# Attention products with the values as stationary operand, two heads side by side, and the softmax sums inverted once per attention

## The reference

```python
def one(qblk):                                   # first attention ("mla"), per 128 queries
    sc = einsum('bqhd,bkhd->bhqk', qblk, k) * scale
    p = softmax(sc, axis=-1)
    return einsum('bhqk,bkhd->bqhd', p, v)
...
s_win = s_win * scale + bias                     # second ("na"): a window of the tokens, and the context
p = softmax(concatenate([s_win, s_ctx], axis=-1), axis=-1)
return einsum(p_win, v_win) + einsum(p_ctx, vc)
...
ya = (oa * silu(za)) @ w_oa
yb = (ob * silu(zb)) @ w_ob
y = (sigmoid(ga) * ya + sigmoid(gb) * yb) @ w_out
```

## Time and profile before

| | |
|---|---|
| median of 3 runs | 3332.46 us (3329.71 to 3333.55) |
| the profiled execution | 3333.67 us, span 3331.9 us |
| PE busy | 3113.7 us, 93% of the span |
| PE weight loads busy | 2443.1 us, 73% |
| VectorE busy | 1628.2 us, 49% |
| ScalarE busy | 1123.6 us, 34% |
| DMA queue, share of 16 engines | 22.5% |
| chain that ended last | PE 86%, DVE 8%, ACT 3% |

### The profile page before, as it was taken

How to read it: one execution, slowest core, us unless ns; L and a number is a source line. 1 busy time by engine, 2 the same in 40 slices (tenths; PEclk the granted TensorE clock), 3 DMA queues, 4 the chain that set the end, 5 groups by cost and what they waited for, 6 DMA issues and landing times.

```text
span 3331.9 us, 38502 instructions
## 1 busy us (share of the span) xinstructions
PE 3113.7 (93%) x15469; PEld 2443.1 (73%) x15469; DVE 1628.2 (49%) x2719; ACT 1123.6 (34%) x1821; POOL 134.7 (4%) x145
## 2 busy tenths in 40 slices
PE   7999898999999899999999999679999989987998
PEld 6888745666666688887788888458888757877886
DVE  5434544555556554344743345765535435245335
ACT  3322223434344333233332233543323333233332
POOL 0000001211111100000000000000000000100000
PEclk9999899999999899999999999789999979987999
DMA  4333221111100133332233322013233210301231
GB/s 129 94 96 101 78 74 45 46 42 34 53 17 20 64 95 95 102 95 93 84 96 96 100 90 72 1 44 95 89 102 97 59 29 1 93 7 48 88 93 61
DMA packets 186183, 234.76 MB, mean 70 GB/s; under 512 B 14201, under 2 KB 127446, under 8 KB 185750
## 3 DMA queue, kind: packets, MB, share of 16 engines
q1 hardware_dynamic: 186006, 232.29, 22.5%
HBM read 228.05 MB, written 4.19 MB: 70 GB/s over the span
## 4 chain that ended last, share of the span: by engine, by line
PE 86%; DVE 8%; ACT 3%; issue 2%; POOL 1%; SPq 0%; DMA 0%; DVEq 0%; ACTq 0%
PE banks L866 61%; PE banks L991 3%; PE banks L1370 3%; PE banks L1023 2%; PE banks L977 1%; PE banks L1364 1%; PE banks L1358 1%; PE banks L1014 1%; PE banks L1058 1%; PE banks L1087 1%; PE banks L1083 1%; PE banks L955 1%; DVE diff_scores L2378 1%; DVE diff_small L2384 1%; PE banks L1032 1%
## 5 line engine op out<-in xcount | busy, mean ns | idle before, releaser
L1922 DVE TENSOR_TENSOR weights_lo<-weights_raw,weights_hi 128x1024 fp32r<-128x1024 f32 (+3 forms) x377 | 453.1, 1205 | 999.1 <-ACT weights_hi L1441 997.6
L866 PE MATMUL banks<-operand_hi,weights_hi 128*128 128x512 f32 x2080 | 822.6, 395 | 34.5 <-DVE weights_lo L1922 13.0
L866 PE MATMUL banks<-operand_hi,weights_lo 128*128 128x512 f32 x2080 | 815.8, 392 | 0.0
L866 PE MATMUL banks<-operand_lo,weights_hi 128*128 128x512 f32 x2080 | 815.8, 392 | 0.0
L1441 ACT ACTIVATE weights_hi<-weights_raw 128x1024 fp32r<-128x1024 f32 (+3 forms) x377 | 391.2, 1041 | 1060.4 <-PE banks L866 1030.1
L866 PEld LDWEIGHTS banks<-operand_hi,weights_hi 128*128 128x128 f32 x2080 | 394.1, 189 | 124.4 <-issue 27.2
L866 PEld LDWEIGHTS banks<-operand_lo,weights_hi 128*128 128x128 f32 x2080 | 394.4, 190 | 83.7 <-issue 2.2
L866 PEld LDWEIGHTS banks<-operand_hi,weights_lo 128*128 128x128 f32 x2080 | 393.9, 189 | 83.3
L866 PE MATMUL banks<-hidden_ffn_hi,weights_hi 128*128 128x512 f32 x352 | 137.1, 390 | 0.0
L866 PE MATMUL banks<-hidden_ffn_lo,weights_hi 128*128 128x512 f32 x352 | 136.9, 389 | 0.0
L866 PE MATMUL banks<-hidden_ffn_hi,weights_lo 128*128 128x512 f32 x352 | 136.9, 389 | 0.0
(11 more groups left out here) (519 smaller groups left out, 4520.5 us busy)
## 6 DMA issues: line engine op xcount, KB each, us to landing
weights_raw<-in_ffn_w_in_dram SPq DMA_DIRECT2D x352, 256.0 KB, 3.1
weights_raw<-in_ffn_w_out_dram SPq DMA_DIRECT2D x88, 512.0 KB, 3.8
weights_raw<-in_w_in_dram SPq DMA_DIRECT2D x36, 512.0 KB, 3.6
weights_raw<-in_rwkv_w_rkv_dram SPq DMA_DIRECT2D x24, 512.0 KB, 3.9
weights_raw<-in_w_mod_dram SPq DMA_DIRECT2D x24, 512.0 KB, 4.9
weights_raw<-in_w_kv_dram SPq DMA_DIRECT2D x16, 512.0 KB, 3.6
weights_raw<-in_rwkv_w_o_dram SPq DMA_DIRECT2D x8, 512.0 KB, 5.1
weights_raw<-in_diff_w_q_dram SPq DMA_DIRECT2D x8, 512.0 KB, 4.8
```

Of the source, the lines that this page charges most:

```text
L866: mm = nc.tensor.matmul(o, l, r, start=first and t == 0 and job["opens"], stop=last and t == 2, **skip)
L1922: nc.vector.tensor_tensor(ring_lo[0:p, u["slot"], 0:n, 0:w], ring_raw[0:p, u["ring"], 0:n, 0:w], f32(ring_hi[0:p, u["slot"], 0:n, 0:w]), A ...
```

## The change

For lanes 0 and 2, step 4 handles two heads: the values of a head (64 columns) are the stationary operand and the turned probabilities (128 queries) stream past them. The even lane's head goes to partitions 0 to 63 of bank A, the odd lane's to 64 to 127 of the same bank, alternating from matmul to matmul. The output comes out turned already, unscaled, and one 128x128 copy stores the two heads. Odd lanes have no step 4. Copies of turned probabilities go to VectorE for even lanes and to ScalarE for odd lanes, whatever `tb`. The row sums are kept for all heads and blocks and inverted by one instruction after each attention. In place of the 16 transpositions per z come 32 products that spread the inverted sums over 64 partitions each; VectorE multiplies the output by silu(z) and then by them.

```diff
+        def turned_by(lane, tb):
+            return lane_act if lane % 2 else lane_dve
...
-                        if tb:
+                        if lane % 2 == 0 and tb:
                             pe.wait_ge(*lane_dve[lane].at((name, "o", hd, tb - 1)))
...
-                    elif s == 4:
-                        pe.wait_ge(*(lane_act if tb % 2 else lane_dve)[lane].at((name, "turned", hd, tb)))
+                    elif s == 4 and lane % 2 == 0:
+                        for e in range(2):
+                            pe.wait_ge(*turned_by(lane + e, tb)[lane + e].at((name, "turned", hd + e, tb)))
                         for kt in range(KEY_TILES):
-                            mm = nc.tensor.matmul(ps[:, A, 0:MLA_V], turned_[:, lane, kt * P:(kt + 1) * P],
-                                                  value(hd, kt), start=kt == 0, stop=kt == KEY_TILES - 1)
+                            for e in range(2):
+                                mm = nc.tensor.matmul(ps[e * HEAD:(e + 1) * HEAD, A, 0:P], value(hd + e, kt),
+                                                      turned_[:, lane + e, kt * P:(kt + 1) * P], start=kt == 0,
+                                                      stop=kt == KEY_TILES - 1, skip_group_check=True)
...
+                    if k == 0:
+                        pe.wait_ge(*sums_inverted.at(name))
                     for tb in range(TB):
-                        mm = nc.tensor.transpose(ps[:, jobs[job]["bank"], tb * P:(tb + 1) * P],
-                                                 o_all[:, tb, k * P:(k + 1) * P], ident[:, :])
-                    mm.then_inc(*gate_turned.by((z, k)))
+                        for e in range(2):
+                            mm = nc.tensor.matmul(ps[e * HEAD:(e + 1) * HEAD, jobs[job]["bank"], tb * P:(tb + 1) * P],
+                                                  attn_sums[name][:, 2 * k + e, tb:tb + 1].broadcast_to([P, HEAD]),
+                                                  ident[:, :], start=True, stop=True)
+                    mm.then_inc(*gate_spread.by((z, k)))
...
                         nc.scalar.activation(probs_[:, lane], flat[:, 0:KEYS], ACT.Exp, bias=sm[:, 1:2], scale=scale,
-                                             accum_out=sm[:, 2:3]).then_inc(*lane_act[lane].by((name, "exp", hd, tb)))
-                    elif s == 3 and tb % 2:
+                                             accum_out=attn_sums[name][:, hd, tb:tb + 1]).then_inc(...)
+                    elif s == 3 and turned_by(lane, tb) is lane_act:
...
-                    elif s == 2:
-                        dve.wait_ge(*lane_act[lane].at((name, "exp", hd, tb)))
-                        nc.vector.reciprocal(sm[:, 3:4], sm[:, 2:3]).then_inc(*own.by((name, "rs", hd, tb)))
-                    elif s == 3 and tb % 2 == 0:
+                    elif s == 3 and turned_by(lane, tb) is lane_dve:
...
-                    elif s == 4:
+                    elif s == 4 and lane % 2 == 0:
                         dve.wait_ge(*lane_pe[lane].at((name, "o", hd, tb)))
-                        dve.wait_ge(*own.at((name, "rs", hd, tb)))
-                        nc.vector.tensor_scalar(o_all[:, tb, hd * MLA_V:(hd + 1) * MLA_V], ps[:, A, 0:MLA_V], sm[:, 3:4],
-                                                None, ALU.mult).then_inc(*own.by((name, "o", hd, tb)))
+                        nc.vector.tensor_copy(o_all[:, hd // 2, tb * P:(tb + 1) * P],
+                                              ps[:, A, 0:P]).then_inc(*own.by((name, "o", hd, tb)))
+
+            def invert_sums(name):
+                sums = attn_sums[name].rearrange("p h b -> p (h b)")
+                nc.vector.reciprocal(sums, sums).then_inc(*sums_inverted.by(name))
...
-                    nc.vector.tensor_tensor(gtmp[:, k % 2], ps[:, jobs[job]["bank"]], z_[:, k],
+                    nc.vector.tensor_tensor(gtmp[:, k % 2], o_all[:, k], z_[:, k], ALU.mult).then_inc(*dve_own.by())
+                    dve.wait_ge(*dve_own.now())
+                    dve.wait_ge(*gate_spread.at((z, k)))
+                    nc.vector.tensor_tensor(gtmp[:, k % 2], gtmp[:, k % 2], ps[:, jobs[job]["bank"]],
                                             ALU.mult).then_inc(*evac_d.by(job))
```

More of the change, by code:

```diff
@@ L579, in attention_plan @@
                 elif s == 2:
-                    lane_dve[lane].expect((name, "rs", hd, tb))
                     lane_pe[lane].expect((name, "turn", hd, tb))
                 elif s == 3:
-                    (lane_act if tb % 2 else lane_dve)[lane].expect((name, "turned", hd, tb))
-                else:
+                    turned_by(lane, tb)[lane].expect((name, "turned", hd, tb))
+                elif lane % 2 == 0:
                     lane_pe[lane].expect((name, "o", hd, tb))
@@ L598, in program @@
         close("na")
-        gate_turned = signal("gate_turned", [(z, k) for z in "ab" for k in range(4)])
+        sums_inverted = signal("sums_inverted", ["mla", "na"])
+        gate_spread = signal("gate_spread", [(z, k) for z in "ab" for k in range(4)])
         for z in "ab":
@@ L638, in program @@
         mod, gain = sb("modulation", [P, 24, 2]), sb("mod_gain", [P, KC, 2])
-        attn_small = sb("attn_small", [P, LANES, 4])
+        attn_small = sb("attn_small", [P, LANES, 2])
+        attn_sums = {name: sb(f"{name}_sums", [P, MLA_HEADS, TB]) for name in ("mla", "na")}
         vecs = sb("vectors", [P, 256])
@@ L730, in program @@
                 mod_tmp = sb("mod_tmp", [P, 3, T], on=ph2)
-            o_mla = sb("mla_out", [P, TB, T], on=ph)
+            o_mla = sb("mla_out", [P, MLA_HEADS // 2, T], on=ph)
             with ExitStack() as ph2:
@@ L745, in program @@
                                  sb("mla_probs_turned", [P, LANES, KEYS], on=ph2))}
-            o_na = sb("na_out", [P, TB, T], on=ph)
+            o_na = sb("na_out", [P, NA_HEADS // 2, T], on=ph)
             with ExitStack() as ph2:
@@ L1352, in attention @@
                     if s == 0:
-                        if tb:
+                        if lane % 2 == 0 and tb:
                             pe.wait_ge(*lane_dve[lane].at((name, "o", hd, tb - 1)))
-                        elif hd >= LANES:
+                        elif lane % 2 == 0 and hd >= LANES:
                             pe.wait_ge(*lane_dve[lane].at((name, "o", hd - LANES, TB - 1)))
@@ L1395, in pe_program @@
             fence("na")
-            for z, o_all in (("a", o_mla), ("b", o_na)):
+            for z, name in (("a", "mla"), ("b", "na")):
                 dense_pass("z" + z, op, lambda k: op_lo.at(("h", k)))
@@ L1834, in attention @@
                         nc.scalar.activation(probs_[:, lane], flat[:, 0:KEYS], ACT.Exp, bias=sm[:, 1:2], scale=scale,
-                                             accum_out=sm[:, 2:3]).then_inc(*lane_act[lane].by((name, "exp", hd, tb)))
-                    elif s == 3 and tb % 2:
+                                             accum_out=attn_sums[name][:, hd, tb:tb + 1]).then_inc(*lane_act[lane].by((name, "exp", hd, tb)))
+                    elif s == 3 and turned_by(lane, tb) is lane_act:
                         act.wait_ge(*lane_pe[lane].at((name, "turn", hd, tb)))
@@ L2544, in dve_program @@
             fence("mla")
+            invert_sums("mla")
             for n in ("kb", "vb", "qb"):
@@ L2551, in dve_program @@
             fence("na")
-            for z in "ab":
+            invert_sums("na")
+            for z, o_all in (("a", o_mla), ("b", o_na)):
                 convert_all("z" + z)
                 for k, job in enumerate(block_jobs["turn_z" + z, 0]):
-                    dve.wait_ge(*gate_turned.at((z, k)))
                     dve.wait_ge(*ready_at("z" + z, k))
```

## The result

| | us | ratio to before, with its 95% interval |
|---|---|---|
| before | 3332.59 (3329.71 to 3333.55) | |
| changed | 3287.43 (3282.35 to 3290.76) | 0.9865 [0.9848, 0.9882] |
| changed, second measurement | 3292.96 | 0.9872 [0.9858, 0.9887] |
| changed, third measurement | 3291.76 | 0.9873 [0.9859, 0.9886] |

The forecast was 3295, in a range of 3284 to 3314. The kernel before, measured beside each of the three, took 3332.59, 3332.85 and 3333.74 us, so the gain is 45.2 us, 39.9 and 42.0; 37.6 was forecast.

A forecast was written before the change was run, and what follows sets the result against it. First-attention rounds were taken as TensorE's work end to end; the second also had an idle gap and low clock. From 3333.67: -20.6 - 21.2 + 0.1 + 4.1 = -37.6, 3296.1; median 1.2 lower, 3295; range 3284 to 3314.

The forecast's parts named there:

- The value products: Values of each round: 64-column loads alternating between array halves, 0.054 us a record, 48 records in 2.62 us, not 5.4.
- rival 3: Value products: halves take turns, 0.109 us a record, kernel slower at 3347; worst case by the skill's rule 3397; chance 0.05.
- The first attention: Its rounds were to fall from 13.93 to 11.35 us, 2.58 each, 20.6 us for eight.
- the 0.3 us for the change of shape: First attention: cost per round of changing TensorE's tile shape around the value products, about 0.3 us.
- The gates and stores: Spreading products replacing transpositions add 4.1 us in both z; the last store of each attention adds 0.05.
- The second attention: Its rounds were to fall from 17.10 to 14.45 us, 2.65 each, 21.2 us for eight.
- The rows speak for the middle: Second attention: the clock rises by the time the values run, as before, giving 14.45 us rounds between 13.1 and about 17.
- rounds of 14 to 15 us: Sign expected in the profile after: length of a round of the second attention.
- a mean clock not above 0.85: Sign expected in the second attention's clock row, with falls to 0.50 as before.
- Rival 1: Second attention: clock stays high, rounds of 13.1 us, 32 us saved in place of 21.2, about 3284; chance 0.12.
- Rivals 2, 3 and 4: Second: second attention's clock stays low longer, 3316, chance 0.12. Third: halves take turns, 0.05. Fourth: nothing moves, 3332, 0.03.

The follow-up runs named there:

- `one_half`: Changed kernel with both heads' results in partitions 0 to 63, so one half of the array is used: 3339.68 us (1.0013).
- the filled kernels: Changed kernel and kernel before, each with seven extra products per second-attention round in TensorE's gap behind the scores: 3284.38 and 3324.34 us.
- `halves_in_turn`: Changed kernel with loops over key tiles and heads exchanged, six products of one head, then six of the other: 3317.96 us (0.9947).
- `pairs_in_turn`: Changed kernel with the two pairs of lanes half a round apart in the second attention: 3282.8 us (0.9849).
- `after_third`: The changed kernel unaltered, run a third time for comparison on one chip: 3291.76 us (0.9873).
- `gates_plain`: Changed kernel without the spreading products and the second multiplication in the gates: 3286.85 us (0.9854).

## Why the prediction was right

**The value products** (48 records in 2.62 us from start to start): 2.84 less a tail of 0.27 is 2.57. The prices came from L1245 and L1176, and both the pairing and its need for two halves are shown by `one_half`. The rule of the Trainium skill (TensorE: Matmul & The Clock Gate, Part 3) that a load overlaps running products only if it is for other rows, from which rival 3 had its worst case, doesn't describe this case: 48 loads and 48 streams over all rows cover 2.84 us.

**The first attention** (20.6 us): 21.4. Every time of the round was met within 0.1 us, and the 0.3 us for the change of shape with it.

**The gates and stores** (4.2 us): 4.4, of which the gates are 2 x (3.86 - 1.8) = 4.1, 1.8 being the 16 transpositions that they replace.

**The second attention** (21.2 us) came to 28.3, and here the prediction was off in size. The step that failed is "The rows speak for the middle: 5.1 us of unbroken work preceded the rise in the round shown, and that work is unchanged". The work is unchanged, but the clock rose 3.6 us after the transpositions began, not 5.1 or more, and the values started at 10.74 where 11.5 to 11.6 was forecast. That step also counted the low stretch from the start of the transpositions, though it had begun in the gap before them. I had taken one alignment of the low stretch with the round as if it belonged to the round; when the round's length changed, the alignment did, and in `one_half` it changed between equal rounds. Two of the signs that the prediction named were missed by this: rounds of 14 to 15 us (13.56) and a mean clock not above 0.85 (0.87). What sets the place of the low stretch stays open. The mechanism that the filled kernels measure, 2.8 us a round for the products, would have given 22.5, close to the forecast; the other 0.7 a round is the clock. Rival 1 had the right argument, that the idle time falls in another place of the round when its length changes, but not its case: the clock did fall, in all eight rounds, for less time.

**Rivals 2, 3 and 4** fell: the clock was higher, the records go in pairs, and the round followed TensorE.

**The clear misses among the expectations** were `halves_in_turn`, 12.74 us a round where 13.9 was expected (the profile of before had a hint, L1148, which I named there only in favour of the rival), and `pairs_in_turn`, 3282.8 us where 3263 to 3276 was expected. The rival of `after_third`, that the second attention's time varies with its start through the clock, fell in that run but holds in `gates_plain`: a start at 2749.2 and 109.9 us.

## What to carry to other kernels

When a product's result is only 64 wide, making the 64-wide operand stationary pays, in f32 as here, only if two such products run in the two halves of the array, and in full only if they alternate; look for a place in the same kernel that has this form and take the price from there. Count what the shorter stage uncovers: here the copies, hidden before, were worth 4.7 us in the first attention as soon as the products were paired. And where the clock changes within a repeated round, compute the round with the clock held at either level and give the place of its fall and its rise as unknown; it moves with the round's length, and even between equal rounds.

## What the runs showed of the hardware

- Two f32 products with 64-column stationary tiles in different halves of the array run side by side, 0.054 us a record at full clock; in one half they take 0.110 each.
- The overlap needs no strict alternation: at a change of half about 3.5 records (0.38 us) of the two overlap.
- Behind an idle gap of 3.35 us the clock was low for 3.4 us, from the start of the transpositions, in one kernel, and for at least 6.7 us, from 1.1 us before them, in another. In two neighbouring rounds of `one_half`, with the same work and a gap of 3.48 us in both, it was low for 6.8 us of the one (17.13 us) and at 1.00 all through the other (15.79 us).
- The same instructions take up to 12 us more or less before the first attention from one execution to the next (first score at 2737.1 to 2749.2), while the stages behind it repeat to 0.1 us in three profiles of the changed kernel and differ by 1.5 us in a fourth with the same instructions (`gates_plain`). The cause stays open.
